# One attention and gated-linear-attention backbone on one Trainium2 core: the layer boundary in halves, output stores by quarter, two weight casts moved, and a head's probabilities turned in three groups with the prompt's scores inside the second

## The reference, cut to what matters

```python
xn   = rmsnorm(x, norm_w) * (1.0 + scale) + shift     # shift, scale, gate from the conditioning vector
proj = xn @ w_in                                      # one projection, cut into the columns of all heads
q, k = rmsnorm(aq), rmsnorm(ak)                       # 8 query heads, 2 key heads, rotary on latents
out_a = softmax(q @ k_all.T * scale) @ v_all * silu(ag)   # a latent query sees 512 latent keys and 128 cached ones,
                                                          # a prompt query the 128 prompt keys
out_b = cb * conv3_centred(cc * ch, conv_w) * silu(cg)
out_c = rmsnorm(gla_bidir(gq, gk, gv, gates)) * silu(gg)  # 4 heads, two directions
x    = x + gate * (concat(out_a, out_b, out_c) @ w_out)
```

## Time and profile before

| what | value |
|---|---|
| runs | 2124.11 us median of 3 (2122.39 to 2124.4) |
| the profiled execution | 2122.44 us |
| its span, first to last instruction | 2120.6 us |
| granted TensorE clock, mean | 0.998 |
| TensorE busy | 2086.0 us, 98% |
| VectorE busy | 1476.1 us, 70% |
| ScalarE busy | 645.8 us, 30% |
| one looped head of attention, from the start of its values' product to that of the next | 38.2 us |

### The profile page before, as it was taken

How to read it: one execution, slowest core, us unless ns; L and a number is a source line. 1 busy time by engine, 2 the same in 40 slices (tenths; PEclk the granted TensorE clock), 3 DMA queues, 4 the chain that set the end, 5 groups by cost and what they waited for, 6 DMA issues and landing times.

```text
span 2120.6 us, 33656 instructions
## 1 busy us (share of the span) xinstructions
PE 2086.0 (98%) x13025; PEld 1853.5 (87%) x13025; DVE 1476.1 (70%) x2915; ACT 645.8 (30%) x1096; POOL 176.4 (8%) x118
## 2 busy tenths in 40 slices
PE   5999999999999999999999999999999999999998
PEld 4788888888999999999988888888899999999998
DVE  5869799998666657866475455566666576687655
ACT  4232221321433334442142222232133333353302
POOL 0000000000000000523210000000000000043331
PEclk9999999999999999999999999999999999999999
DMA  9989687764333324664445547454343233266444
GB/s 370 392 299 342 214 280 253 242 220 157 116 99 104 107 76 138 197 204 141 122 128 175 183 125 220 139 145 143 113 124 107 75 99 107 91 219 203 151 127 145
DMA packets 357334, 365.43 MB, mean 172 GB/s; under 512 B 17670, under 2 KB 264156, under 8 KB 356572
## 3 DMA queue, kind: packets, MB, share of 16 engines
q1 hardware_dynamic: 328528, 320.67, 47.4%
q10 hardware_dynamic: 28684, 43.09, 5.4%
HBM read 304.98 MB, written 58.72 MB: 172 GB/s over the span
## 4 chain that ended last, share of the span: by engine, by line
PE 94%; DVE 2%; ACT 1%; issue 1%; DMA 1%; ACTq 0%; SPq 0%; DVEq 0%
PE psP L916 31%; PE psT L928 8%; PE psP L989 8%; PE psP L984 6%; PE psP L986 6%; PE psP L985 6%; PE psO L998 5%; PE psP L991 4%; PE psT L998 3%; PE psP L1175 3%; PE psO L1221 3%; PE psT L1186 2%; PE psO L958 1%; PE psT L833 1%; DMA wmod<-in_w_mod_dram 0%
## 5 line engine op out<-in xcount | busy, mean ns | idle before, releaser
L916 PE MATMUL psP<-x_pair,high 128*128 128x512 f32 x1704 | 547.9, 391 | 0.0
L916 PEld LDWEIGHTS psP<-x_pair,high 128*128 128x128 f32 x1704 | 319.8, 188 | 71.3 <-issue 4.9
L916 PE MATMUL psP<-x_pair,low 128*128 128x512 f32 x852 | 331.8, 389 | 0.0
L1437 ACT ACTIVATE high<-raw 128x1024 fp32r<-128x1024 f32 x128 | 135.5, 1059 | 588.3 <-PE psT L928 509.9
L1958 DVE SCALAR_TENSOR_TENSOR macc<-mraw,cond,macc 128x128 f32<-128x128 f32 (+1 forms) x810 | 308.6, 455 | 0.0
L1976 DVE TENSOR_TENSOR low<-raw,high 128x1024 fp32r<-128x1024 f32 x128 | 157.1, 1228 | 173.2 <-ACT high L1437 173.1
L989 PE MATMUL psP<-x_pair,high 128*128 128x512 f32 x512 | 200.9, 392 | 0.0
L916 PEld LDWEIGHTS psP<-x_pair,low 128*128 128x128 f32 x852 | 160.0, 188 | 32.9 <-issue 0.5
L984 PE MATMUL psP<-x_pair,high 128*128 128x384 f32 x512 | 180.2, 352 | 0.0
L986 PE MATMUL psP<-x_pair,low 128*128 128x384 f32 x512 | 172.2, 336 | 0.0
L985 PE MATMUL psP<-x_pair,high 128*128 128x384 f32 x512 | 171.7, 335 | 0.0
(11 more groups left out here) (348 smaller groups left out, 4029.1 us busy)
## 6 DMA issues: line engine op xcount, KB each, us to landing
raw<-in_w_in_dram SPq DMA_DIRECT2D x132, 512.0 KB, 5.3
wmod<-in_w_mod_dram SPq DMA_DIRECT2D x32, 1024.0 KB, 8.9
mraw<-in_w_mod_dram SPq DMA_DIRECT2D x64, 512.0 KB, 4.2
mraw<-in_w_mod_dram SPq DMA_DIRECT2D x32, 1024.0 KB, 7.0
raw<-in_w_in_dram SPq DMA_DIRECT2D x32, 1024.0 KB, 5.6
raw<-in_w_out_dram SPq DMA_DIRECT2D x64, 512.0 KB, 4.0
old<-x_scratch SPq DMA_DIRECT2D x64, 320.0 KB, 2.9
xf<-proj_scratch SPq DMA_DIRECT2D x48, 320.0 KB, 3.4
```

The lines of the kernel that those rows point to most:

```text
L916: mm = pe.matmul(latent_ps[m], own, moved, start=(k == 0 and w is whole and x is x_high), stop=(k == KT - 1 and x is x_low))
L1437: act.activation(ring(high, l, n), ring(raw, l, n), ACT.Copy).then_inc(s["chunk_cast"], 1)
```

## The change

Five things are changed.

1. **Boundary.** The factor of the tokens goes to PSUM in another place, in three steps with a signal each: the first 256 latents, the other 256, the prompt. For tile 0 VectorE scales, and ScalarE shifts, the two halves apart. The last tile's squares of the last 128 latents and of the prompt are made apart as well, each with its signal.
2. **Stores by quarter.** Each of the ten stores of 128 tokens by 1024 columns becomes two of 512 columns, each waiting for the one engine that makes it.
3. **Casts sooner.** In each GLA pair `cast_half(f + 3)` goes ahead of the gate's first activation, `cast_half(f + 4)` to where f + 3 was, and `low_half` alike on VectorE.
4. **Three groups.** A head's 21 transposes go in three groups (8, 7 and 6) where there were five (5, 5, 5, 5 and 1). The first group stands after `score(2)` and has block 0 and three fifths of block 1. ScalarE and VectorE take each group in two pieces, 6 and 5 in a head where they were 5 and 4.
5. **The prompt's scores in the second.** `score(4)` goes from its own place in the `psP` bank into the end of `psT`, ahead of the second group.

```diff
+SPREAD, SUMMED, SQUARES = 256, 5, KT + 1
...
+PROMPT_AT = 7 * P
+TURNS = (((0, 0, 5, 0), (1, 0, 3, 5)), ((2, 0, 5, 0), (1, 3, 5, 5)), ((3, 0, 5, 0), (TT - 1, 0, 1, 5)))
+TAKES, LOWS = sum(len(parts) for parts in TURNS), sum(len(parts) for parts in TURNS) - 1
+TURNED_FOR = (0, 0, 1, 2, 2)
+MAX_STEP, SCALE_STEP = (1, 3, 5, 7, 8), (2, 4, 6, 9, 10)
...
+        prompt_score = psT[:, PROMPT_AT:PROMPT_AT + SEQ]
...
+        def rstd_ps(part):
+            return psT[:, 512:512 + SEQ] if part.start == DEC else psO[:, 512 - SPREAD + part.start:512 - SPREAD + part.stop]
...
-            for i in range(TT):
-                for side in range(2):
-                    part = slice(side * D // 2, (side + 1) * D // 2)
-                    sp.wait_ge(s["x_taken"], KT + 2 * i + side + 1)
-                    sp.wait_ge(s["y_scaled"], KT + 2 * i + side + 1)
-                    dst = io["y_sample"][0, i * P:(i + 1) * P, part] if i < TT - 1 else io["y_prompt"][0][:, part]
-                    sp.dma_start(dst, ytok[:, i, part]).then_inc(s["y_out"], 16)
-            sp.wait_ge(s["y_out"], 16 * TT * 2)
+            for u in range(TT * 4):
+                i, part = u // 4, slice(u % 4 * 512, (u % 4 + 1) * 512)
+                sp.wait_ge(s["y_scaled" if u % 2 else "x_taken"], KT + u // 2 + 1)
+                dst = io["y_sample"][0, i * P:(i + 1) * P, part] if i < TT - 1 else io["y_prompt"][0][:, part]
+                sp.dma_start(dst, ytok[:, i, part]).then_inc(s["y_out"], 16)
+            sp.wait_ge(s["y_out"], 16 * TT * 4)
...
-                        if i >= DEC // P - 1:
+                        if i in (SPREAD // P - 1, DEC // P - 1, TT - 1):
...
-                                mm = pe.matmul(score_ps[:, 0:SEQ], qw[:], key[:, g, DEC:TOK], start=True, stop=True)
+                                mm = pe.matmul(prompt_score, qw[:], key[:, g, DEC:TOK], start=True, stop=True)
                             mm.then_inc(s["scored"], 1)
-                        def turn(i):
-                            pe.wait_ge(s["probs_scaled"], hd * TT + i + 1)
-                            pe.wait_ge(s["pt_copied"], hd * TT + i + SEED)
-                            pe.wait_ge(s["pt_low"], hd * (TT - 1) + i + SEED)
-                            for j in range(KEYS // P if i < TT - 1 else 1):
-                                mm = pe.transpose(psT[:, j * P:(j + 1) * P], probs[i % 2][:, j * P:(j + 1) * P], ident[:])
+                        def turn(n):
+                            pe.wait_ge(s["probs_scaled"], hd * TT + (2, 3, TT)[n])
+                            pe.wait_ge(s["pt_copied"], hd * TAKES + 2 * n + SEED)
+                            pe.wait_ge(s["pt_low"], hd * LOWS + 2 * n + SEED)
+                            if n == 1:
+                                score(TT - 1)
+                            for i, first, last, at in TURNS[n]:
+                                for j in range(first, last):
+                                    to = (at + j - first) * P
+                                    mm = pe.transpose(psT[:, to:to + P], probs[i % 2][:, j * P:(j + 1) * P], ident[:])
                             mm.then_inc(s["prob_turned"], 1)
...
-                        for i in range(1, TT):
+                        for i in range(1, TT - 1):
                             part = i + 2 if begun else i + 1
                             project_quarter(part // 4, part % 4, n)
                             score(i)
-                            turn(i - 1)
+                            if i > 1:
+                                turn(i - 2)
                         if begun:
+                            project_quarter(1, 2, n)
                             project_part(1, KT * 3 // 4, KT - 1, n)
-                            turn(TT - 1)
+                            turn(2)
                             project_part(1, KT - 1, KT, n)
                         else:
+                            project_quarter(1, 1, n)
                             project_quarter(1, 2, n)
-                            turn(TT - 1)
+                            turn(2)
                             project_quarter(1, 3, n)
-                        pe.wait_ge(s["pt_copied"], hd * TT + TT + SEED)
-                        pe.wait_ge(s["pt_low"], (hd + 1) * (TT - 1) + SEED)
+                        pe.wait_ge(s["pt_copied"], (hd + 1) * TAKES + SEED)
+                        pe.wait_ge(s["pt_low"], (hd + 1) * LOWS + SEED)
...
-                        for v in range(2):
-                            shift_part(0, v)
-                            shift_part(1, v)
+                        act.wait_ge(s["scaled"], KT + 1)
+                        act.activation(x_high[:, 0, 0:SPREAD], xt[0][:, 0:SPREAD], ACT.Identity, bias=mod[:, 0, 0:1])\
+                            .then_inc(s["shifted"], 1)
+                        act.wait_ge(s["scaled"], KT + 2)
+                        act.activation(x_high[:, 0, SPREAD:DEC], xt[0][:, SPREAD:DEC], ACT.Identity, bias=mod[:, 0, 0:1])\
+                            .then_inc(s["shifted"], 1)
+                        shift_part(1, 0)
+                        shift_part(0, 1)
+                        shift_part(1, 1)
...
                         prob(1)
+                        if not squared:
+                            take_tile(0)
                         act.wait_ge(s["pv_done"], hd + SEED)
                         take(0)
-                        if not squared:
-                            take_tile(0)
-                        for i in range(2, TT):
-                            prob(i)
-                            take(i - 1)
+                        prob(2)
+                        take(1)
+                        prob(3)
+                        prob(4)
                         for k in range(4) if last else ():
                             mix_high(k)
-                        take(TT - 1)
+                        take(2)
...
                     cast_half(f + 1)
+                    cast_half(f + 3)
...
-                    cast_half(f + 3)
+                    cast_half(f + 4)
                     keep_sum(f + 1)
...
-                    cast_half(f + 4)
...
-                for done, n, part, squared in (("left_step", 4 * l + 2, slice(0, LEFT), "left_step"),
-                                               ("taken1", OUT_PAIRS + occ + SECOND + SEED, slice(LEFT, TOK), "x_sq")):
+                for done, n, part, squared in (("left_step", SUMMED * l + 2, slice(0, LEFT), "left_step"),
+                                               ("left_step", SUMMED * l + 5, slice(LEFT, DEC), "x_sq"),
+                                               ("taken1", OUT_PAIRS + occ + SECOND + SEED, slice(DEC, TOK), "x_sq")):
...
-                    for v in range(2):
-                        dve.wait_ge(s["stat_summed"], 3 * l + v)
-                        for k in range(2):
-                            scale_part(k, v)
+                    for cols, n in ((slice(0, SPREAD), 1), (slice(SPREAD, DEC), 2)):
+                        dve.wait_ge(s["stat_summed"], 2 * l + n)
+                        dve.scalar_tensor_tensor(xt[0][:, cols], xf[:, 0, cols], mod_a[:, 0, 0:1], rstd_ps(cols),
+                                                 ALU.mult, ALU.mult).then_inc(s["scaled"], 1)
+                    scale_part(1, 0)
+                    dve.wait_ge(s["stat_summed"], 2 * l + 3)
+                    for k in range(2):
+                        scale_part(k, 1)
...
-                        def prob_low(i):
-                            dve.wait_ge(s["pt_copied"], hd * TT + i + 1 + SEED)
-                            dve.tensor_tensor(probs_low[:, :, i * P:(i + 1) * P],
-                                              psT[:, 0:KEYS].rearrange("p (a b) -> p a b", b=P),
-                                              probs_high[:, :, i * P:(i + 1) * P].bitcast(F32), ALU.subtract)\
-                                .then_inc(s["pt_low"], 1)
+                        def probs_lows(n):
+                            parts = [part for part in TURNS[n] if part[0] < TT - 1]
+                            dve.wait_ge(s["pt_copied"], hd * TAKES + 2 * n + 2 + SEED)
+                            for i, first, last, at in parts:
+                                dve.tensor_tensor(probs_low[:, first:last, i * P:(i + 1) * P],
+                                                  psT[:, at * P:(at + last - first) * P].rearrange("p (a b) -> p a b", b=P),
+                                                  probs_high[:, first:last, i * P:(i + 1) * P].bitcast(F32), ALU.subtract)\
+                                    .then_inc(s["pt_low"], 1)
...
                         for i in range(TT):
                             if i == (1 if split_ahead else 2):
                                 right_sum(0)
-                            row_max(i)
-                            if i < 2:
-                                if not split_ahead:
-                                    split_quarter(1, i + 2, n, hd)
-                            else:
```

(16 more changed lines are left out.)

67 lines of the change are left out of this document (34 added, 33 removed).

## The result

The changed kernel takes 2129.52 us (median of 8 runs, 2128.49 to 2133.24), the kernel before 2124.24 (8 runs, 2122.39 to 2125.37): a ratio of 1.0029, 95% interval 1.002 to 1.0038. It was forecast at 2124.8, within 2121.0 to 2128.0. It lies above the range, and it is slower where no measurable change was the forecast. The profiled execution's span is 2126.5 us, 5.9 above that of before.

A forecast was written before the change was run, and what follows sets the result against it. TensorE's work was taken as the bound, busy 2086.0 of 2120.6 us. 2122.44 -0.3 +2.0 -0.8 -0.7 -0.15 +0.6 = 2123.1 us profiled; with runs' median 1.67 above that, 2124.8, range 2121.0 to 2128.0.

The forecast's parts named there:

- The other heads: Heads after a layer's first: transposes in three groups make TensorE wait nowhere, cost nothing, with 0.8 us slack at block 2's division.
- rival 2: Looped heads wait at their second group for block 2's division, 0.35 us in each of 14: 4.9 us, 2129.7; chance 0.07.
- a pitch of 38.5: Sign in the new trace: looped heads 38.5 us apart, instead of staying at 38.2, would speak for rival 2.
- The first head: First head of each layer: TensorE's values' product waits 1.0 us for VectorE's low part; two layers, +2.0 us.
- Three groups: Transposes in three groups: two visits fewer in each of 16 heads save 0 to 1.2 us, taken as 0.3.
- Casts: First GLA pair: casts sooner remove a 0.4 us wait between turn_keys(0) and fill(4); two layers, -0.8 us.
- Boundary: Between the layers: tile 0 in halves gives -0.5 us, with the squares cut in two -0.7 together.
- The squares' 0.2: Between the layers: squares cut in two, the first run while VectorE works, and fewer sums behind save about 0.2 us.
- The squares and the first store at the end: End of layer 2: the same cut of the squares saves 0.15 us.
- Stores: Tail of stores: packets halved from 4 KB to 2 KB move 400 GB/s instead of 420, +0.6 us, bounds 0 and +1.2.

The follow-up runs named there:

- load_ahead: Changed kernel with ScalarE's two waits before each exponential exchanged, the maximum's last, putting looped heads' table load ahead of it: 2124.29 us, 1.0001 of before.
- load_behind: Kernel before with the same two ScalarE waits exchanged, putting looped heads' table load behind the maximum's wait: 2128.63 us, 1.0021 of before.
- best_three: first_head with the last stores by halves as before: 2120.62 us, 0.9985 of before.
- best_five: old_turns with stores by halves, no q_n wait, and the table load ahead of the maximum's wait in all heads: 2119.74 us, 0.9984 of before.
- three_busy: best_three with two more idle TensorE products (keep_busy 6 for 4) ahead of the factor's spreading: 2120.84 us, 0.9983 of before.
- five_busy: best_five with two more idle TensorE products (keep_busy 6 for 4) ahead of the factor's spreading: 2119.07 us, 0.9980 of before.
- first_head: all_ahead with the first head's last transpose group one projection step earlier: 2121.35 us, 0.9990 of before.
- old_turns: Kernel before with the boundary, casts and stores edits, keeping five groups and the prompt's scores in their old place: 2122.46 us, 0.9996 of before.
- all_ahead: load_ahead without the q_n wait and, in heads outside a loop, the maximum's wait first: 2123.24 us, 0.9998 of before.

## Why the prediction was wrong, step by step

**The other heads** is the step that failed: "I cost these at nothing, and this is what hides it." I placed VectorE's new list ahead of the division, and that was right: block 2 was divided 0.75 us before TensorE was done with score 3 (664.20 + 0.55 against 665.50; forecast slack 0.8), so that rival 2 didn't come. The sign that I had named for rival 2, a pitch of 38.5, did come, from another cause. I followed two engines of three. ScalarE's table load was in the order of both kernels, with its wait, and I looked at ScalarE's copies alone. In its place the runs showed a table load behind its wait that costs TensorE 0.42 us in each of 12 heads with three groups (38.51 against load_ahead's 38.09) and 0.34 with five (load_behind's 38.52 against 38.18). In the changed kernel 0.09 of it is covered by what three groups save, and 0.33 a head is left, 4.0 in the trace. At the medians the exchange gave 5.2 (4.6 with before's own shift taken out) and 5.0. The heads are 12, two layers of six: the last head of a layer is not in a loop, where I had counted 14, and its load stood behind the wait before as well, so it took 38.52 before and 38.45 now. It is a rival that I didn't name: the slower side was among my rivals, with another mechanism.

**The first head** was right in place, releaser (VectorE's low part, by the rows above) and size: 0.99 us per layer, 2.0 in the list of waits, 1.9 given back by one step of the projection.

**Three groups** were right in kind and sized low: -0.09 us in each looped head (38.09 against 38.18), 1.1 us over 12 heads, where I took 0.3 of 0 to 1.2. But best_three and best_five show that the gain is given back. Against best_five's 268.06 the heads take 267.5, 0.56 less a layer. From the projection to the first head's values, however, three_busy has 485.85 and five_busy 485.34: 0.5 more, of which first_head's row shows 0.3 as a wait. That leaves 0.1 us in all; the medians even say 0.9 and 1.8 the other way, which I can't place.

**Casts**: the stall behind the keys went. TensorE in the first pair after, as the earlier trace rows:

```profile
866.34 0.76 PE L1281 MATMUL psT<-ident,kt_ 128*128 128x128 f32 x5
866.86 0.83 PE L1009 MATMUL psO<-x_pair,high 128*128 128x384 f32 x4
```

0.52 where it was 0.92 (0.89 in the second layer), as forecast. In layer 0 of this execution 0.4 came back 100 us later, at the output's norm, which is a chain of small steps. VectorE in the second pair, after, and GpSimd at the same time:

```profile
963.47 1.16 DVE L2438 TENSOR_SCALAR var_o<-sums_o 128x10 f32<-128x10 f32 x1
...
966.48 0.74 DVE L1855 SCALAR_TENSOR_TENSOR tmp_o<-r_o 128x10 f32<-128x10 f32 x1 [0.72 <-ACT r_o L1420]
```

```profile
963.35 1.26 POOL L2545 TENSOR_TENSOR ct<-cu,vecs 128x641 f32<-128x641 f32 x1 [0.17 <-POOL ct L2552]
964.68 2.50 POOL L2556 TENSOR_TENSOR ct<-ct 128x641 f32<-128x641 f32 x1
```

Before, these two took 0.58 and 0.17. Each long one ends 0.02 to 0.04 us after an instruction of GpSimd does: 964.63 after 964.61, and 967.22 after 967.18; before, 961.98 after 961.96. It is so in all 14 traces, for each of these two steps that takes longer than 0.18: it starts while an instruction of GpSimd runs, ends just behind it, and takes up to 1.16 us. So what came back is the wait for GpSimd, and how long that is depends on where GpSimd's own chain happens to stand. In old_turns and best_five nothing came back (256.0 against 256.4), so this is not the casts' own price.

**Boundary**: 0.53 for the 0.5 of the halves. The squares' 0.2 lies in the table's row before: from the first of the last sums to the group that the table counts from it took 1.31 us before and 1.04 after. From that first sum to the projection it took 6.22 and takes 5.42, 0.8 for the forecast 0.7. **The squares and the first store at the end**: 0.15 forecast, 0.11 shown (4.14 to 4.03 from sums to store). **Stores**: +0.6 forecast, +1.2 in the traces and 1.0 between two kernels of one set, at my upper bound. The rate of 392 GB/s alone gives 13.4 us for 5.24 MB, +0.9; the other 0.3 lie at the two ends of the tail. The 400 GB/s that I took from the loads at the start fits the part in which only stores run (404 to 407 in after's windows); the 377 to 383 while the other engines work is what I hadn't counted, and what causes it was not tested. The estimate from the Trainium skill's page "DMA: Bandwidth & Descriptors", section "Why small descriptors are slow (HBM only)" (+0.3) was lower still.

Row by row of the table, with the stretches that it leaves out, the two spans differ by: -0.55 before the first head (the start, bound by loads, which the change doesn't touch), +1.05 and +1.39 at the two first heads, +4.01 in the other heads, -0.56 in GLA and the squares, -0.53 at the boundary, -0.11 at the last sums, +1.19 in the tail: 5.9. Of the 1.39, 0.99 are the wait at the values. Most of the rest is the third row of the waits after: at layer 1's first head the table load started 0.36 us after `nm` was there, where it took 0.07 before and takes 0.07 in layer 0. It stood behind its wait in both kernels, so this isn't the cause told above, and the trace doesn't show what it is.

## What to carry to other kernels

Where an activation function changes, look at what stands ahead of the table load: the wait for the data should stand behind it. Which of several waits travels with the activation is decided when the kernel is compiled, and a change of a counter's step somewhere else can turn it round. When a change renumbers the semaphores of a loop, read the compiled order of every engine with its waits, not only of the two that the change is about. Three engines pass a head on from hand to hand here, and the loss came from the third.

## What the runs showed of the hardware

- The table load took 1283 ns in the mean of every group that the views list, in each of the kernels looked at. The Trainium skill's page "ScalarE activation tables: per-element evaluation and per-set limits", section "What a function is on this engine", gives the same figure, and "ScalarE: Activation LUTs", section "Step-by-step: what each stage is for", says about 2.7 us including a drain. No such drain shows here: in the row of all_ahead the 16 loads have 0.3 us of idle time ahead of them in all, and after the load that ends at 653.87 the exponential starts at 653.88. In front of a wait the load cost nothing, and behind it 1.3 us of latency, of which TensorE felt 0.34 to 0.42.
- The granted clock fell to 0.50 (1.2 GHz) after a wait of TensorE of only 0.32 us with small products on both sides, in 3 of 12 profiles of kernels that have it; at this place it cost 1.6 us with the new boundary (6.01 for 4.38) and 1.1 with the old (6.03 for 4.91).
- A VectorE step of 10 columns, which takes 0.17 us, took up to 1.16 when it was begun while GpSimd ran an instruction of the convolution, and ended 0.02 to 0.04 us after that instruction did, in all 14 traces. No run changes GpSimd's part, so it is the alignment of the two that shows it.
- Writing 256 KB pieces in 2 KB packets ran at 377 to 383 GB/s beside working compute engines and at 404 to 407 alone, 392 in the mean; 512 KB pieces in 4 KB packets ran at 420 in both. The transfer engines were full in all of them.

The best version is five_busy, five groups with the boundary in halves, the casts sooner, the stores by halves and the table load ahead of its wait: 0.9980 of before (0.9970 to 0.9989), 4.6 us. best_five, best_three and three_busy are within its interval.
